# Four heads' values token by token, and the second half of the last norm by rows, in a one-core decoder kernel

## What is computed

```python
proj = rmsnorm(h, kv_norm_g) @ w_kv
k, v, f_logit = jnp.split(proj, [D_INNER, 2 * D_INNER], axis=-1)
cum = jnp.cumsum(log_sigmoid(f_logit + b_forget), axis=1)
...
q, r = jnp.split(rmsnorm(h, norm_g) @ w_in, 2, axis=-1)
s = q @ k.T + cum[q rows] - cum[k columns]       # causal, per head, q scaled
o = softmax(s) @ v
h = h + (o * silu(r)) @ w_out
return rmsnorm(h, final_norm_g)[:, N_META:]
```

## Time and profile before

| | us |
|---|---|
| three timed runs: median (lowest, highest) | 1025.69 (1025.11, 1025.74) |
| the profiled execution's own time | 1027.1 |
| its span in the trace | 1025.3 |
| TensorE busy in the span | 1013.7 |
| VectorE, ScalarE, GpSimd busy | 638.4, 521.8, 34.3 |
| mean granted TensorE clock | 0.996 of full |

### The profile page before, as it was taken

The page is one execution under the profiler, slowest core; times in us unless marked ns, Lnnn a source line. Parts: engine busy times, 40 slices in busy tenths (PEclk is TensorE's granted clock), DMA queues, the critical chain, the costliest instruction groups (busy, mean ns, idle before and its releaser), DMA issues.

```text
span 1025.3 us, 18641 instructions
## 1 busy us (share of the span) xinstructions
PE 1013.7 (99%) x7655; PEld 950.4 (93%) x7655; DVE 638.4 (62%) x1100; ACT 521.8 (51%) x932; POOL 34.3 (3%) x69
## 2 busy tenths in 40 slices
PE   8999999999999999999999999999999999999997
PEld 7999999999999999998999999999999999988886
DVE  6875666577567784447665656655656566576433
ACT  6754644654474553336554545454545555564321
POOL 0000000000000000000101000000000000010000
PEclk9999999999999999999999999999999999999998
DMA  8221221221122122222444333332434332331312
GB/s 286 70 77 63 83 84 49 76 83 64 62 87 79 63 70 96 91 96 65 135 110 89 110 89 86 94 102 89 110 97 102 104 94 77 99 87 67 119 42 82
DMA packets 34838, 92.98 MB, mean 91 GB/s; under 512 B 3888, under 2 KB 12976, under 8 KB 34752
## 3 DMA queue, kind: packets, MB, share of 16 engines
q1 hardware_dynamic: 34320, 91.62, 29.3%
q10 hardware_dynamic: 432, 0.15, 0.1%
HBM read 89.43 MB, written 2.13 MB: 89 GB/s over the span
## 4 chain that ended last, share of the span: by engine, by line
PE 98%; DMA 1%; DVE 0%; ACT 0%; issue 0%; DVEq 0%; SPq 0%; ACTq 0%
PE psum L1385 81%; PE psum L1701 3%; PE psum L1510 2%; PE psum L1684 2%; PE psum L1438 1%; PE psum L1458 1%; PE psum L1672 1%; PE psum L1671 1%; PE psum L1673 1%; PE psum L1506 1%; PE psum L1479 1%; DMA hT<-xT 1%; PE psum L1689 1%; PE psum L1504 0%; PE psum L1436 0%; PE psum L1408 0%
## 5 line engine op out<-in xcount | busy, mean ns | idle before, releaser
L820 DVE TENSOR_TENSOR w_lo<-raw,w_hi 128x1024 fp32r<-128x1024 f32 x143 | 173.5, 1223 | 28.4 <-ACT w_hi L431 28.3
L431 ACT ACTIVATE w_hi<-raw 128x1024 fp32r<-128x1024 f32 x143 | 149.6, 1052 | 34.8 <-PE psum L1385 34.1
L1385 PE MATMUL psum<-xh,w_hi 128*128 128x264 f32 x768 | 159.1, 288 | 2.7 <-DVE xl L842 1.5
L1385 PE MATMUL psum<-xl,w_hi 128*128 128x264 f32 x768 | 155.9, 285 | 0.0
L1385 PE MATMUL psum<-xh,w_lo 128*128 128x264 f32 x768 | 155.3, 283 | 0.0
L1385 PEld LDWEIGHTS psum<-xh,w_hi 128*128 128x128 f32 x768 | 118.5, 189 | 4.2 <-issue 2.3
L1385 PEld LDWEIGHTS psum<-xl,w_hi 128*128 128x128 f32 x768 | 119.5, 188 | 0.0
L1385 PEld LDWEIGHTS psum<-xh,w_lo 128*128 128x128 f32 x768 | 119.1, 189 | 0.0
L1385 PE MATMUL psum<-zh,w_hi 128*128 128x264 f32 x512 | 106.0, 288 | 0.0
L1385 PE MATMUL psum<-y_lo,w_hi 128*128 128x264 f32 (+2 forms) x400 | 104.8, 314 | 0.0
L1385 PE MATMUL psum<-zl,w_hi 128*128 128x264 f32 x512 | 104.0, 285 | 0.0
(11 more groups left out here) (266 smaller groups left out, 1851.3 us busy)
## 6 DMA issues: line engine op xcount, KB each, us to landing
raw<-w_all SPq DMA_DIRECT2D x143, 512.0 KB, 3.3
sub<-sums SPq DMA_DIRECT2D x16, 264.0 KB, 7.1
sub<-sums SPq DMA_DIRECT2D x16, 200.0 KB, 6.5
sub<-sums SPq DMA_DIRECT2D x16, 136.0 KB, 4.7
hT<-xT SPq DMA_DIRECT2D x8, 264.0 KB, 6.7
outT<-hT SPq DMA_DIRECT2D x8, 256.0 KB, 2.5
sub<-sums SPq DMA_DIRECT2D x16, 72.0 KB, 3.5
raw<-w_all SPq DMA_DIRECT2D x2, 256.0 KB, 5.1
```

The lines of the kernel that those rows point to most:

```text
L431: nc.scalar.activation(w_hi[:, n % HI_RING, :], raw[:, n % LO_RING, :], ACT.Copy).then_inc(hi_made, 1)
L820: nc.vector.tensor_tensor(w_lo[:, n % LO_RING, :], raw[:, n % LO_RING, :], w_hi[:, n % HI_RING, :].bitcast(F32), ALU.subtract).then_inc(lo ...
L1385: i = nc.tensor.matmul(o, w[a][:, k % KT, :], x[b][:, k, c0:c1], start=k == first and a == b == 0, stop=k == last and a == 1)
```

## The change

- **Values in groups of four heads.** `v` and `x` jobs are gone. For each of four groups g there is one job `u{g}`: 8 k-tiles by 4 blocks of 128 tokens by 3 products, 96 matmuls, in which the activations `zh`/`zl` (128 tokens) are stationary and the weights of four heads (512 columns) move. It fills PSUM banks 4 to 7, one for each block, token by feature at once, so nothing is turned. ScalarE and VectorE then write `fv_hi` and `fv_lo` from the banks in the order 3, 2, 0, 1 (`U_ORDER`). `u{g}` stands after attend(4g-1); `u0` after `q0`.
- **The 16 last tokens** get a job `m{g}` of their own (`end_values`): 8 fp32 matmuls of 512 columns with 16 output rows, in four groups of partitions as in `LOWF`, with the unsplit weights in `raw` moving. So VectorE may write `w_lo` of the group's first chunk over `raw` only after `m{g}`. ScalarE copies three parts, VectorE sums them, and both write `fv_end`.
- **The residual** leaves for DRAM (`h_keep`, eight stores of 256 KB from `hT` during the projection `W`), since `fv_hi`/`fv_lo` of four heads now lie over `hT`, and comes back after attend(15) by eight loads ahead of the load of chunk `w4b`.
- **Two or three k-tiles of `r{h}`** now stand ahead of scores(h): three for the first head of a group, else two. Scores(h) of a group's first head wait block by block for `fvlo_made`.
- **The last norm's second half** is turned: while the root is made, TensorE transposes the scaled residual into rows, 128 tokens by 1024 features in two PSUM banks for each of two blocks, and ScalarE and VectorE each multiply one bank of a block by the inverse root of its token (a column now) and the rows are stored, ScalarE's from its own queue. The diagonals, the spreading matmuls and the four multiplications of this half are gone. The host puts the two halves of the output together.

```diff
-        + ["k0", "LOWF", "q0", "v0", "x0", "v1"] + [j for h in range(FOX_HEADS) for j in fox_step(h)] + [f"w{d}" for d in range(KT)])
+        + ["k0", "LOWF", "m0", "q0", "u0"] + [j for h in range(FOX_HEADS) for j in fox_step(h)] + [f"w{d}" for d in range(KT)])
...
+            keep = {CHUNK[f"W{d + 1}b"] + LO_RING: d for d in range(1, KT - 1)}
+            keep.update({CHUNK["W1b"] + LO_RING: 0, CHUNK["k0"] + LO_RING: KT - 1})
...
+                if n in keep:
+                    d = keep[n]
+                    sp.wait_ge(h_made, d + 1)
+                    sp.dma_start(h_keep[:, d, :], hT[:, d, META:T]).then_inc(h_kept, 16)
+                if n == CHUNK["w1b"] + LO_RING:
+                    done(sp, f"a{FOX_HEADS - 1}")
+                    for d in range(KT):
+                        sp.dma_start(hT[:, d, META:T], h_keep[:, d, :]).then_inc(h_back[d], 16)
                 load(n)
...
+            def end_values(g):
+                job = f"m{g}"
+                wait_slot(pe, job)
+                pe.wait_ge(z_end_made, 1)
+                for part in range(VH):
+                    n = CHUNK[f"u{g}{part}"]
+                    pe.wait_ge(w_loaded[n % LO_RING], 16 * (n // LO_RING + 1))
+                for k in range(KT):
+                    r = 32 * (k % 4)
+                    w = raw[:, CHUNK[f"u{g}{k // 2}"] % LO_RING, :].rearrange("p (k n) -> p k n", k=2)
+                    i = nc.tensor.matmul(bank(slot(job), 0, VH * P, r, r + META), z_end[:, k, :], w[:, k % 2, :], start=k < 4, stop=k >= 4)
+                i.then_inc(job_done, 1)
...
+            def fox_values(g):
+                if g:
+                    pe.wait_ge(alo_made, 4 * VH * g)
...
+                for part in range(VH):
+                    n = CHUNK[f"u{g}{part}"]
+                    pe.wait_ge(lo_made, n + 1)
...
+                    for k in (2 * part, 2 * part + 1):
+                        for b in range(NBLK):
+                            for a, p in ((0, 0), (0, 1), (1, 0)):
+                                i = nc.tensor.matmul(bank(4 + b), xk[a][:, k, b * BLK:(b + 1) * BLK], w[p][:, k % 2, :], start=k == a == p == 0,
+                                                     stop=k == KT - 1 and a == 1)
...
             for h in range(H):
-                if h + 1 < H:
-                    fox_scores(h)
-                    strip_late(f"r{h}", xq)
...
+                n = 3 if h % VH == 0 else 2
...
+                late_part(f"r{h}", range(0, n))
+                fox_scores(h)
+                late_part(f"r{h}", range(n, KT)).then_inc(job_done, 1)
...
-                if h + 1 < H:
-                    pe.wait_ge(fvt_made, h + 2)
-                    transposed(f"x{h + 1}", fvt)
-                if h + 2 < H:
-                    strip(f"v{h + 2}", xk)
+                if last:
+                    fox_values((h + 1) // VH)
...
-            last_sums(1, acc, True, False)
+            pe.wait_ge(scaled, KT - 1)
+            turned(0, 0, KT - 1)
...
-            last_spread(1)
+            pe.wait_ge(scaled, KT + 1)
+            turned(0, KT - 1, KT).then_inc(tail_turned, 1)
+            turned(1, 0, KT).then_inc(tail_turned, 1)
```

More of the change, by code:

```diff
@@ L148, in program @@
         eps = eps_all[:, 0:1]
-        hT = sb("hT", [P, KT, T])
+        with ExitStack() as one:
+            hT = sb("hT", [P, KT, T], F32, one)
+        fv_hi = sb("fv_hi", [P, NBLK, VH * P], F32R)
+        fv_lo = sb("fv_lo", [P, NBLK, VH * P], F32R)
+        sb("h_rest", [P, KT * T - 2 * NBLK * VH * P])
         with ExitStack() as one:
@@ L256, in slot, with end_groups @@
             return PLACE[job]
+        TURNED = (PLACE[f"w{KT - 2}"], 6)
+        SPREAD, SUMMED = PLACE[f"w{KT - 1}"], (4, 5)
+        def end_groups(g):
+            i = 8 if g < NBLK - 1 else 12
+            return [y[0:META, i + n, 0:VH * P] for n in range(4)]
         def joined(b):
             return psum[:, (b + 1) * BANK - BLK:(b + 1) * BANK + T - BLK]
+        h_keep = nc.dram_tensor("h_keep", (P, KT, SEQ), F32, kind="Internal").ap()
         sums = nc.dram_tensor("sums", (FOX_HEADS, T), F32, kind="Internal").ap()
@@ L349, in wait_chunk_used @@
             name = CHUNKS[n]
-            if name[0] not in "Ww":
+            if name[0] == "u":
+                g, part = int(name[1]), int(name[2])
+                if part < VH - 1:
+                    eng.wait_ge(u_used, (VH - 1) * g + part + 1)
+                else:
+                    eng.wait_ge(job_done, JOB[f"u{g}"] + 1)
+            elif name[0] not in "Ww":
                 eng.wait_ge(job_done, JOB[name] + 1)
@@ L683, in queries_hi, with end_groups_out, end_values_hi, fox_values_hi @@
                 nc.scalar.activation(fq_hi[:], fkf[:, 0:SEQ], ACT.Copy).then_inc(qhi_made, 1)
[L685 to L688, removed]
-                else:
[L690 to L695, removed]
+            def end_groups_out(g):
+                done(act, f"m{g}")
+                for n, part in enumerate(end_groups(g)[1:]):
+                    r = 32 * (n + 1)
+                    nc.scalar.activation(part, bank(slot(f"m{g}"), 0, VH * P, r, r + META), ACT.Copy).then_inc(end_copied, 1)
+            def end_values_hi(g):
+                if g:
+                    done(act, f"a{VH * g - 1}")
+                else:
+                    act.wait_ge(stack_zeroed, 3)
                 act.wait_ge(rtok_made, 4)
[L697 to L700, removed]
+                act.wait_ge(end_sum, 3 * (g + 1))
                 for r in (R_HI, R_MID):
[L702 to L705, removed]
+                    nc.scalar.activation(fv_end[r:r + META, :], end_groups(g)[0], ACT.Copy, scale=rtok[0:META, NBLK:NBLK + 1]).then_inc(end_hi, 1)
+            def fox_values_hi(g):
+                done(act, f"u{g}")
+                act.wait_ge(rtok_made, 4)
+                if g == 0:
+                    act.wait_ge(h_kept, 16 * KT)
+                for b in U_ORDER:
+                    nc.scalar.activation(fv_hi[:, b, :], bank(4 + b), ACT.Copy, scale=rtok[:, b:b + 1]).then_inc(fvhi_made, 1)
             def softmax(h):
@@ L1244, in _ @@
             fox_key(0)
+            done(dve, "m0")
+            ahead(f"W{KT - 1}b")
             x = slot("LOWF")
@@ L1297, in _ @@
                     z_low(0, 4)
+                elif g is not None:
+                    done(dve, f"m{g}")
+                    ahead(f"r{h}")
+                    ahead(f"k{h + 1}")
                 elif h + 1 < H:
@@ L1651, in _, with sums_by_token @@
-            strip("v1", xk, sums_by_token)
+            rstd_by_token(slot("m0") + 1)
+            def sums_by_token():
+                pe.wait_ge(f_cum, 1)
+                pe.wait_ge(rtok_made, 4)
+                for b in range(NBLK):
+                    i = nc.tensor.transpose(bank(slot("m0") + 1, CUM_AT + FOX_HEADS * b, CUM_AT + FOX_HEADS * (b + 1)),
+                                            fb[:, META + BLK * b:META + BLK * (b + 1)], ident[0:FOX_HEADS, 0:FOX_HEADS])
+                i.then_inc(cum_done, 1)
@@ L1735, in _ @@
                 transpose_probs(h)
+                last = h + 1 < H and (h + 1) % VH == 0
+                if last:
+                    end_values((h + 1) // VH)
                 if h + 1 < H:
```

328 lines of the change are left out of this document (198 added, 130 removed).

## The result

The changed kernel takes **1031.87 us** (median of 6 runs, 1031.09 to 1032.62) against 1025.72 (6 runs, 1025.11 to 1026.23) for the kernel before: a ratio of 1.006, 95% interval 1.005 to 1.007. It is slower by 6 us, where 5 us less was forecast, and lies outside the range of 1017.0 to 1024.0. The execution profiled for this took 1032.07 us.

A forecast was written before the change was run, and what follows sets the result against it. TensorE's own work was taken as the bound. From 1027.1 us, -4.4 (values), +1.0 (first scores) and -1.8 (tail) gave 1021.9 profiled; with the median 1.4 lower, 1020.5 us was predicted, range 1017.0 to 1024.0.

The forecast's parts named there:

- the fourth of the waits costed at nothing: Projection: residual's loads issued at the end of attend(15), first needed after 5.5 us, landing in 3.3 us; no cost.
- A new wait takes the gain: Rival, 12%: fourth chunk lands late or `u`'s eviction is held up behind splits; +2 to +3.5 us, so 1023.3.
- The sign that I had named for being wrong: In the heads: TensorE waits above 2 us in sum would show the forecast wrong.
- `u`: Added TensorE work per group of four heads: 96 matmuls of 512 columns at the `r` strip's pace, 22.5 us.
- columns alone: Rival, 3%: each matmul costs only its columns at 2.4 GHz, `u` takes 20.5 us; 1012.5 us.
- The faster pace: Rival, 15%: `u` runs at the output projection's 0.2294 us a matmul and TensorE never waits at the groups; 1018 us.
- `m`: Added TensorE work per group for the 16 last tokens, priced by columns from `LOWF`: 1.94 us.
- Slower than before: Rival, 5%: the four partition groups of `m` don't overlap at 512 columns; +14.2 us, 1034.7 us.
- A group's first scores: Block 3's scores wait for VectorE to finish all four value banks: 0.25 us in each of four groups, +1.0 us.
- The fourth chunk: Its load, queued behind the spreading of sums, lands before `m{g}` needs it, with 0.8 us of cover; no cost.
- The change from attend to the strip: Between attend(h) and scores(h+1), in three of four heads: six matmuls of `r` at 1.4 us, no extra cost.
- The two other covers: `k0`'s eviction before `q0`, just covered, else 0.2 us; attend's eviction before scores, covered by 0.5 us.

The follow-up runs named there:

- the run without waits: Changed kernel with residual loads ahead of `w3b`, spreading of sums behind each group's fourth chunk, four k-tiles before a group's first scores: 1020.95 us.

## Why the prediction was wrong

**The step that failed** is the fourth of the waits costed at nothing: that the residual's loads "are issued at the end of attend(15)", so that 5.5 us of matmuls cover 3.3 us of transfer. The wait for attend(15) in the diff is on SyncE, and I took the time of that wait for the time of the issue. What stands ahead of it in the same queue waits longer: the load of `w3b`, for the end of `w0`. Issue came 6.6 us after attend(15). Landing then took 6.6 us and not 3.3, since two chunks went ahead (4.5 us with one). The code shows this without a run: every load names the chunk six places back, whose use is the release, so the placement ahead of `w4b` (ring place of `w1b`) reads as "after `w3b`, which waits for all of `w0`". And `w0`'s end is what the addition waits for anyway, so the addition has no cover left, and TensorE has 12 matmuls of `w1`, 2.8 us, before it needs the bank. The rival *A new wait takes the gain* had the kind right, but its price (2 to 3.5 us) and its places (the fourth chunk, the eviction of `u`) were other ones; the fourth chunk did wait, and is the smaller part. The two runs with other places for the loads show it: 7.2 and 3.2 us back. The sign that I had named for being wrong, waits above 2 us in the heads, was there too (1.5 + 0.7), but stood for the smaller part.

**The clock** was no term of mine in the projection. The changed kernel shows 1.3 us of it, the profiled execution with 2.88 us of idle time none.

**`u`** at 22.5 us: measured 22.47. The pace of the `r` strip was the right row, and not that of the projection (22.0) or the columns alone (20.5). *The faster pace* and *columns alone* fall.

**`m`** at 1.94 us: 1.84 to 1.94. The four groups of partitions overlap at 512 columns as at 264. *Slower than before* by 14 us falls; the kernel did get slower, but from elsewhere.

**A rule weighed.** On switches of the tiling mode, the Trainium skill says in "TensorEngine Tiling (Array Packing)", Key Properties, that changing it drains TensorE. No run here shows a drain by itself, and whatever it is has no weight: in the run without waits the transposes ahead of `m1` take 1.51 us to its start, as they do ahead of a `q`, and the `q` behind it takes 5.71 us, as behind transposes (5.70 to 5.71).

**A group's first scores** at +0.25 us: measured +0.43, so 1.7 and not 1.0 us. This term was mis-sized. VectorE kept its pace of 0.66 us from start to start but ended the last bank 3.65 us after `u` (612.92 to 616.57) and not 3.5, mainly since ScalarE's first copy took 0.69 us and not 0.60; TensorE was ready for block 3 after 3.37 us and not 3.25. So block 3 starts 0.33 us late, 0.17 of which the list of waits names, and the last 0.1 comes behind it. With one k-tile more all of it is gone.

**The fourth chunk** (the first of the waits costed at nothing): the cover was put at 0.8 us and was -0.6 in head 3 and -1.0 at worst. TensorE was ready for `m1` 11.6 us after the scores' end, as costed (568.69 to about 580.25). But the last mask on GpSimd stood at 579.56, 10.9 after it, where 9.8 had been read from the earlier trace rows, and the chunk came 12.1 after it and not 10.8. It cost 1.8 us in all. A cover of 0.8 us read from one instance is not a cover.

**The change from attend to the strip**, at nothing: six matmuls of `r` between attend(h) and the scores take 1.48 to 1.50 us and not 1.40, in each of twelve heads. That is 1.1 us that the forecast didn't have: the first of them takes 0.32 us and not 0.23 behind attend's last product. No experiment was made on it.

**The two other covers** held: `q0` followed `m0` at 467.38 without a wait for `k0`'s eviction, and two k-tiles cover attend's eviction.

**The end** at -1.8 us: -1.6 in the trace, -1.6 in the medians of the run that has it alone. The stores bind, as forecast, and the clock stayed at its full level in the transposes. The working had one reading wrong: the two multiplications ahead of the reciprocal stood there before as well, and what came new is one scaling of 0.35 us. Its 1017.95 is 0.33 us after the 1017.62 before, not the 0.1 beside it; counted from the first sums the reciprocal came 0.06 us later.

**The chances**: half of the waits' 12% is 6 and not 4, so the sum is 89 and not 87.

The sum, then: of the 10.2 us, the residual is 7.0, the fourth chunk 1.8, the first scores 0.7, the six matmuls after attend 1.1, the end 0.2, and -0.6 remains, `u` and `m` at their measured prices (-0.2), the start (-0.2) and what no row names.

## What to carry to other kernels

A transfer put into an ordered queue is issued when the slowest of the waits ahead of it is over, not when its own is: for each, write down the release of the load in front of it, and count the bytes ahead of it into its landing. Covers under 1 us read from one instance should be priced as open, and one more k-tile of independent work ahead of a dependent product is the cheap way to close them. A gain of a few us made of many matmuls is lost by one idle stretch at the wrong place, so look at the new transfers of a change before its arithmetic.

## What the runs showed of the hardware

After 5.44 us in which TensorE stood, its granted clock was 0.50 for about 3 us of work, which cost 1.3 us; it had fallen before TensorE started again (0.87 in the window 952 to 953). After 2.88 us at the same place it stayed at 1.00 in the one execution that was profiled. At the end of the changed kernel, with the transposes around the one-column sums, it was 1.00 in every window until TensorE had nothing left to do; before, with gaps there, it was 0.50 from 1018 on.

A 256 KB load issued behind two chunks of 512 KB was used 6.6 us after its issue, behind one 4.5 us, behind none at the latest 5.6 us (when the addition, which waited for TensorE, began). A chunk issued 2.9 us after the first of a spreading's four loads, each replicated over 128 partitions, landed 7.7 us after its issue, where the median of all chunks is 3.3 us; with the chunk ahead of the four loads TensorE had no wait for it.
